# A streaming encoder step on one core: the FFN output projection in four passes, two of them by block products, and the post-norm weight applied where x is updated

## The reference

```python
def swiglu(x, w_gate, w_up, w_down):
    a = jnp.einsum('btd,df->btf', x, w_gate)
    b = jnp.einsum('btd,df->btf', x, w_up)
    return jnp.einsum('btf,fd->btd', jax.nn.silu(a) * b, w_down)
...
        ff_a = swiglu(rms_norm(x, g[0]), w['ffn_w_gate'][l, 0], w['ffn_w_up'][l, 0], w['ffn_w_down'][l, 0])
        x = x + 0.5 * rms_norm(ff_a, g[1])
```

## Time and profile before

| what | value |
|---|---|
| median of 3 runs | 1930.51 us (1930.42 to 1939.18) |
| span of the profiled execution | 1930.4 us |
| matmuls | 15888 |
| PE busy | 1912.4 us (99%) |
| DVE busy | 1299.6 us (67%) |
| ACT busy | 1060.2 us (55%) |
| POOL busy | 196.3 us (10%) |
| TensorE clock granted, mean | 0.997 |

### The profile page before, as it was taken

How to read it: one execution, slowest core, us unless ns; L and a number is a source line. 1 busy time by engine, 2 the same in 40 slices (tenths; PEclk the granted TensorE clock), 3 DMA queues, 4 the chain that set the end, 5 groups by cost and what they waited for, 6 DMA issues and landing times.

```text
span 1930.4 us, 38306 instructions
## 1 busy us (share of the span) xinstructions
PE 1912.4 (99%) x15888; PEld 1861.9 (96%) x15888; DVE 1299.6 (67%) x1716; ACT 1060.2 (55%) x2077; POOL 196.3 (10%) x221
## 2 busy tenths in 40 slices
PE   9999999999999999999999999999999999999997
PEld 9999999999669999999999999999997999999997
DVE  7876784574673887578539775883567487758834
ACT  7563665531684656366545653665438556536652
POOL 0000000200352100000020000001236200000011
PEclk9999999999999999999999999999999999999999
DMA  4323323232311222333322223233341222232231
GB/s 161 104 73 107 110 90 97 99 105 77 123 45 45 62 93 83 96 108 109 92 86 77 99 77 121 88 105 96 107 123 41 73 64 99 78 121 89 103 98 65
DMA packets 63627, 177.90 MB, mean 92 GB/s; under 512 B 7569, under 2 KB 16097, under 8 KB 63329
## 3 DMA queue, kind: packets, MB, share of 16 engines
q1 hardware_dynamic: 61328, 167.66, 26.4%
q0 software_dynamic: 2128, 7.80, 1.2%
HBM read 168.26 MB, written 5.36 MB: 90 GB/s over the span
## 4 chain that ended last, share of the span: by engine, by line
PE 94%; DVE 4%; issue 1%; ACT 1%; DMA 0%; POOL 0%; DVEq 0%; ACTq 0%; SPq 0%
PE psum L796 29%; PE psum L794 29%; PE psum L795 29%; PE psum L1129 1%; PE psum L1115 1%; PE psum L1248 1%; DVE y L1952 1%; PE psum L1037 1%; PE psum L1231 1%; DVE rstd L1941 1%; PE psum L1092 1%; PE psum L1203 1%; DVE xlo L2030 0%; DVE w_lo L648 0%; PE psum L1081 0%
## 5 line engine op out<-in xcount | busy, mean ns | idle before, releaser
L794 PE MATMUL psum<-xhi,w_hi 128*128 128x272 f32 x1632 | 473.9, 290 | 0.2
L796 PE MATMUL psum<-xhi,w_lo 128*128 128x272 f32 x1632 | 470.4, 288 | 0.0
L795 PE MATMUL psum<-xlo,w_hi 128*128 128x272 f32 x1632 | 469.6, 288 | 0.0
L796 PE MATMUL psum<-h_hi,w_lo 128*128 128x272 f32 x1216 | 351.0, 289 | 0.0
L795 PE MATMUL psum<-h_lo,w_hi 128*128 128x272 f32 x1216 | 350.0, 288 | 0.0
L794 PE MATMUL psum<-h_hi,w_hi 128*128 128x272 f32 x1216 | 349.5, 287 | 0.0
L794 PEld LDWEIGHTS psum<-xhi,w_hi 128*128 128x128 f32 x1632 | 307.4, 188 | 3.5 <-issue 2.0
L795 PEld LDWEIGHTS psum<-xlo,w_hi 128*128 128x128 f32 x1632 | 307.2, 188 | 0.5
L796 PEld LDWEIGHTS psum<-xhi,w_lo 128*128 128x128 f32 x1632 | 306.7, 188 | 0.0
L648 DVE TENSOR_TENSOR w_lo<-w_raw,w_hi 128x1024 fp32r<-128x1024 f32 (+1 forms) x214 | 184.3, 886 | 163.5 <-ACT w_hi L645 163.0
L645 ACT ACTIVATE w_hi<-w_raw 128x1024 fp32r<-128x1024 f32 (+1 forms) x214 | 160.9, 770 | 216.0 <-PE psum L796 214.0
(11 more groups left out here) (304 smaller groups left out, 3709.9 us busy)
## 6 DMA issues: line engine op xcount, KB each, us to landing
w_raw<-in_w_gate_up SPq DMA_DIRECT2D x172, 512.0 KB, 4.3
w_raw<-in_w_down SPq DMA_DIRECT2D x96, 256.0 KB, 2.8
w_raw<-in_w_down SPq DMA_DIRECT2D x32, 512.0 KB, 3.6
w_raw<-in_even_in SPq DMA_DIRECT2D x16, 512.0 KB, 4.1
w_raw<-in_odd_in SPq DMA_DIRECT2D x10, 512.0 KB, 4.0
w_raw<-in_w_down SPq DMA_DIRECT2D x32, 128.0 KB, 2.6
w_raw<-in_even_out SPq DMA_DIRECT2D x8, 512.0 KB, 4.2
w_raw<-in_odd_out SPq DMA_DIRECT2D x8, 512.0 KB, 4.4
```

The source lines that it names most:

```text
L794: nc.tensor.matmul(out, s_hi, m_hi, start=first, stop=False, skip_group_check=skip)
L795: nc.tensor.matmul(out, s_hi, m_lo, start=False, stop=False, skip_group_check=skip)
L796: return nc.tensor.matmul(out, s_lo, m_hi, start=False, stop=last, skip_group_check=skip)
```

## The change

In each of the four FFNs:

- The 22 hidden tiles of the output projection are now taken in passes over 4, 6, 6 and 6. The first is as before. The middle two are made of "fold" steps, j = 0 to 7: each does two output tiles over six hidden tiles as a block product of seven products with three tile columns, so 7 x 3 x 3 = 63 matmuls. The steps run in the order of `STEPS`: seven 0 to 6, fold 0 to 3, seven 7 to 12, fold 4 to 7, seven 13 to 17. The last pass over 6 tiles is plain, 16 outputs of 18 matmuls.
- The right-hand factors of a fold step are the hidden pairs and three sums of them. POOL makes these (`fold_sums`, four instructions of 272 columns, in the steps with a pair product of pairs 0 to 5); one of them changes `h_raw` in place. ACT's `pair_high` now waits for the second of the four. ACT then makes the high part of the sums (`fold_high`, after `keep` of T3), and DVE their low part (`fold_low`, 816 columns, after `pair_low`).
- The results of a fold step are added to `y` by DVE (`add_fold`, three per step) and by POOL (`sum_fold`, three per step).
- `hold` copies to `y`. `put` is gone: DVE adds the last pass's outputs to `y` (`add_last`), ACT squares them from there (`last_result`).
- The post-norm weight is no longer applied by ACT; `last_update` scales `y` by weight and reciprocal in one DVE instruction per tile. `after_last_pass` lays out the order around it, and in `first_steps` the sum of the second half's squares is taken by PE three matmuls into the second unit of the first product, and not in its first unit.

```diff
-KDOWN = (6, 12)
...
+PASS = 6
...
+FOLDED = 6
+FOLDS = KD
+STEPS = [("seven", q) for q in range(7)] + [("fold", j) for j in range(4)] + [("seven", q) for q in range(7, 13)] + \
+    [("fold", j) for j in range(4, 8)] + [("seven", q) for q in range(13, SEVEN)]
+NS = len(STEPS)
...
-                [("down", m) for m in range(KD)] + [("seven", q) for q in range(SEVEN_A, SEVEN)] +
-                [("down", KD + m) for m in range(KD)],
+KINDS = {"ffn": [("in", f) for f in range(PLAIN)] + [("first", i) for i in range(4)] + STEPS + [("last", i) for i in range(4)],
...
+            def last_pass(s):
...
+                    last_tiles(s, i, range(PASS - 2))
+                pe.wait_ge(pair_lo, len(PAIRS) * (n + 1))
+                for i in range(4):
+                    last_tiles(s, i, range(PASS - 2, PASS))
+                for i in range(4, 2 * KD):
+                    pe.wait_ge(y_whole, 2 * KD * n + i - 3)
+                    if i == KD + 2:
+                        last_tiles(s, i, range(PASS), lambda: post_first_half(s), 0)
+                    else:
+                        last_tiles(s, i, range(PASS))
...
+            def after_last_pass(c):
+                s, g = c - 1, G0[c]
...
+                split_unit(act, "act", g, 0)
+                last_result(s, 8)
+                last_result(s, 9)
+                post_std(c, 0)
+                split_unit(act, "act", g, 1)
+                for k in range(KD):
+                    act.wait_ge(x_ready, 16 * s + k + 1)
+                    high_part(c, 0, k)
+                    if k in (1, 3, 5):
+                        last_result(s, 10 + k // 2)
+                for i in range(13, 2 * KD):
+                    last_result(s, i)
+                    if i < 15:
+                        for k in range(4 * (i - 13), 4 * (i - 13) + 4):
+                            square(c, 0, k)
+                split_unit(act, "act", g + 1, 0)
...
+            def last_result(s, i):
+                m, H = OUT_ORDER[i]
+                act.wait_ge(y_whole, 2 * KD * ffn_no(s) + i + 1)
+                nc.scalar.activation(scratch[:, m % 4, :], y[:, m, HALF[H]], ACT.Square).then_inc(ysq_ready, 1)
...
             def pair_high(s, p):
-                act.wait_ge(pair_ready, len(PAIRS) * ffn_no(s) + p + 1)
+                if p < FOLDED:
+                    act.wait_ge(fold_made, 4 * (FOLDED * ffn_no(s) + p) + 2)
+                else:
+                    act.wait_ge(pair_ready, len(PAIRS) * ffn_no(s) + p + 1)
                 nc.scalar.activation(h_hi[:, pair_tiles(p), :], h_raw[:, pair_tiles(p), :], ACT.Copy).then_inc(pair_hi, 1)
+            def fold_high(s, p):
+                act.wait_ge(fold_made, 4 * (FOLDED * ffn_no(s) + p) + 4)
+                nc.scalar.activation(fold_hi[:, p % 3].rearrange("p t c -> p (t c)"),
+                                     fold_raw[:, p % 3].rearrange("p t c -> p (t c)"), ACT.Copy).then_inc(fold_high_done, 1)
...
+            def last_update(c, H, between={}):
+                s = c - 1
+                def scaled(j):
+                    for m in (2 * j, 2 * j + 1):
+                        one = y[:, m, HALF[H]]
+                        made = own(nc.vector.scalar_tensor_tensor(out=one, in0=one, scalar=post_gains[:, s, m:m + 1],
+                                                                  in1=rstd[:, HALF[H]], op0=ALU.mult, op1=ALU.mult))
+                    return made
+                n = scaled(0)
+                for j in range(KD // 2):
+                    n_next = scaled(j + 1) if j + 1 < KD // 2 else None
+                    own_wait(n)
+                    two = x[:, 2 * j:2 * j + 2, HALF[H]]
+                    nc.vector.tensor_tensor(two, two, y[:, 2 * j:2 * j + 2, HALF[H]], ALU.add).then_inc(x_ready, 2)
+                    n = n_next
+                    if c < len(SUBS) and j >= 1:
+                        low_part(c, H, 2 * j - 2)
+                        low_part(c, H, 2 * j - 1)
+                    if j in between:
...
+            def add_last(s, i):
+                n, (m, H) = ffn_no(s), OUT_ORDER[i]
...
+                dve.wait_ge(y_ready, y_event(s, m, H) + 1)
+                nc.vector.tensor_tensor(y[:, m, HALF[H]], y[:, m, HALF[H]], psum[:, LAST_BANKS[i % 4], 0:TH],
+                                        ALU.add).then_inc(y_whole, 1)
...
+            def after_last_pass(c):
+                s, g = c - 1, G0[c]
+                add_last(s, 8)
+                if c < len(SUBS):
+                    split_unit(dve, "dve", g, 0)
+                add_last(s, 9)
+                reciprocal(c, True, 0)
+                last_update(c, 0, {j: lambda i=10 + j: add_last(s, i) for j in range(3)})
+                add_last(s, 13)
+                add_last(s, 14)
+                if c < len(SUBS):
+                    split_unit(dve, "dve", g, 1)
+                add_last(s, 15)
+                if c < len(SUBS):
+                    sum_x(c, 0)
+                    split_unit(dve, "dve", g + 1, 0)
+                reciprocal(c, True, 1)
+                if c < len(SUBS):
+                    split_unit(dve, "dve", g + 1, 1)
+                last_update(c, 1)
...
+            def add_fold(s, k, name):
+                j, (corner, right, low) = STEPS[k][1], step_banks(k)
+                m, n = 2 * (j % 4), fold_no(s, k)
+                if j == 0:
+                    dve.wait_ge(first_read, 2 * KD * (ffn_no(s) + 1))
+                elif j >= 4:
+                    dve.wait_ge(fold_added, 3 * (n - 4) + 3)
+                dve.wait_ge(product_done, product_event(s, k, name))
+                if name == "B22":
+                    dve.wait_ge(fold_summed, 3 * n + 2)
+                    nc.vector.tensor_tensor(y[:, m + 1, HALF[0]], psum[:, low, 0:TH], partial[k % 2][:, 0, :],
+                                            ALU.add).then_inc(fold_added, 1)
+                    return
+                one = y[:, m, HALF[0 if name == "B21" else 1]]
+                nc.vector.tensor_tensor(one, one, psum[:, right if name == "B21" else corner, 0:TH],
+                                        ALU.add).then_inc(fold_added, 1)
...
+            def fold_low(s, p):
+                dve.wait_ge(fold_high_done, FOLDED * ffn_no(s) + p + 1)
+                nc.vector.tensor_tensor(fold_lo[:, p % 3], fold_raw[:, p % 3], fold_hi[:, p % 3].bitcast(F32),
+                                        ALU.subtract).then_inc(fold_low_done, 1)
...
+            def fold_sums(s, p):
+                n, (t, u) = 4 * (FOLDED * ffn_no(s) + p), (pair_tiles(p).start, pair_tiles(p).start + 1)
+                left11, left21, left12, left22 = (h_raw[:, i, HALF[H]] for i in (t, u) for H in range(2))
+                sum1, sum2, sum4 = (fold_raw[:, p % 3, i, :] for i in range(3))
+                pool.wait_ge(pair_ready, len(PAIRS) * ffn_no(s) + p + 1)
+                nc.gpsimd.tensor_tensor(sum1, left21, left22, ALU.add).then_inc(fold_made, 1)
+                pool.wait_ge(fold_made, n + 1)
+                nc.gpsimd.tensor_tensor(left21, left21, left11, ALU.subtract).then_inc(fold_made, 1)
+                nc.gpsimd.tensor_tensor(sum2, sum1, left11, ALU.subtract).then_inc(fold_made, 1)
+                pool.wait_ge(fold_made, n + 3)
+                nc.gpsimd.tensor_tensor(sum4, left12, sum2, ALU.subtract).then_inc(fold_made, 1)
+            def sum_fold(s, k):
+                j, n, before = STEPS[k][1], fold_no(s, k), 4 * step_no(s, k)
+                m = 2 * (j % 4) + 1
+                mid, corner = partial[k % 2][:, 0, :], partial[k % 2][:, 1, :]
+                if j == 0:
+                    pool.wait_ge(first_read, 2 * KD * (ffn_no(s) + 1))
+                elif j >= 4:
+                    pool.wait_ge(fold_summed, 3 * (n - 4) + 3)
+                    pool.wait_ge(fold_added, 3 * (n - 4) + 2)
+                pool.wait_ge(kept, before + 2)
+                nc.gpsimd.tensor_tensor(corner, corner, y[:, m, HALF[1]], ALU.add).then_inc(fold_summed, 1)
+                pool.wait_ge(kept, before + 3)
+                nc.gpsimd.tensor_tensor(mid, mid, y[:, m, HALF[0]], ALU.add).then_inc(fold_summed, 1)
+                pool.wait_ge(kept, before + 4)
+                pool.wait_ge(fold_summed, 3 * n + 1)
+                nc.gpsimd.tensor_tensor(y[:, m, HALF[1]], corner, scratch[:, 3, :], ALU.add).then_inc(fold_summed, 1)
+            def ffn_pool(s):
+                for k, (kind, j) in enumerate(STEPS):
+                    if kind == "fold":
+                        sum_fold(s, k)
+                    elif j % 2 == 0 and 0 < j // 2 <= FOLDED:
+                        fold_sums(s, j // 2 - 1)
+                sum_y(s)
```

658 lines of the change are left out of this document (313 added, 345 removed).

## The result

The changed kernel takes 1948.41 us in the median (1948.03 to 1949.22, 4 runs); the kernel before, on the same chip, took 1932.23 us. The ratio of the two is 1.0077, with a 95% interval of 1.0054 to 1.0100. The profiled execution spans 1946.4 us, against 1930.4 before.

The account below looks back on a forecast made before the run. PE, busy 99% of the span, was taken as the bound. From 1930.4 us: matmuls removed -36.0, product steps +36, fold steps +1, between sub-layers +15, the end +1.4, giving 1948 us; range 1910 to 1962.

Follow-up runs that it names:

- e8: Changed kernel with TensorE taking up the total of squares 15 matmuls later at the boundaries; 1945.55 us, 1.0029 to 1.0070 of the kernel before.
- e12: Changed kernel with the post-norm weight left out after each FFN, scaling two tiles an instruction, so another output; 1942.00 us, 1.0037 to 1.0071 of the kernel before.
- e4: Changed kernel with VectorE instead of GpSimd making the four sums right behind the pair's product; 1922.96 us, 0.9931 to 0.9964 of the kernel before.
- e11: Changed kernel with sums on VectorE, their low part moved later, last adds and x's squares moved earlier at boundaries; 1906.72 us, ratio 0.9863 to the kernel before.

## What to carry to other kernels

Before work is given to an idle engine, add what it takes from the busy one: four GpSimd sums of 272 columns took 4.9 us and cost VectorE 0.9, where VectorE makes them in 1.7 by itself. When an engine is near full, what stands ahead of the awaited instruction decides, not the sum of its work: moving one subtract of 0.92 us half a step gained 10 to 13 us, while moving all splits a full step gained 12.5 of the 24 us expected with GpSimd's sums, and cost 5.7 with VectorE's. After moving work, ask when the receiving engine reaches the start of the *next* chain.

## What the runs showed of the hardware

In the changed kernel TensorE's granted clock fell to 0.50 within a stall of 3.16 us, at all three boundaries, and stayed there for about 5 us of matmuls behind it (0.50 in 387 to 392, 1025.1 to 1030 and 1404.3 to 1409.2). The same stall in the nine kernels that leave the boundaries alone, 27 in all, was followed by a mean clock of 0.76 around it 14 times and of 0.88 13 times. A stall of 1.3 us (e8) left the clock at 1.00 each time, one of 2.9 us (e12) at two boundaries of three. So a wait can cost more than its length, here up to 2.2 us of slower matmuls; the boundary as a whole is 0.8 to 1.1 us longer at 0.76 than at 0.88. Windows of e12 at the first boundary, to be set beside those above:

```profile
384.00:387.00 3.00, 0.68 (x5) 0.69 (x6) 2.58 (x3) 1.59 (x4) 2.12 (x2) 1.00 0.41 143
387.00:392.00 5.00, 5.00 (x40) 4.92 (x39) 4.82 (x5) 1.44 (x2) 0.00 (x0) 1.00 0.32 105
```

The other surprise is in the second sub-layer, the even mixer, where the kernels do not differ. From ScalarE's first Exp there to its last it takes 77.5 us in seven of the fourteen traces, 79.1 in three, 80.7 in two and 86.7 in two (e4 and e11). The granted clock in the 20 us behind the first Exp goes with it: 1.00, 0.91, 0.83, and 0.62 to 0.63. These 20 us in the changed kernel and in e11:

```profile
511.97:531.97 20.00, 18.57 (x242) 9.47 (x238) 13.14 (x25) 12.98 (x43) 10.00 (x7) 1.00 0.01 2
```

```profile
500.45:520.45 20.00, 18.57 (x155) 8.59 (x152) 6.58 (x15) 8.74 (x28) 6.45 (x5) 0.63 0.00 1
```

PE issues 155 matmuls there and not 242. The profiled executions of e4 and e11 took 7 us more than their medians (1929.98 and 1913.27); this stretch alone is 9.2 us longer in them than in the changed kernel's. What sets it off I did not test; it is why steps and boundaries are compared here by their own lengths and not by the profiled spans.
